# Second block: where the projections of its second attention, their head norms and its modulation stand in the order

## The reference

```
for l in range(2):
    mod = silu(c) @ w_ada[l] + b_ada[l]                 # 6 * 1024 values
    sh_m, sc_m, gt_m, sh_f, sc_f, gt_f = split(mod, 6)
    h = rms_norm(x, g_mix) * (1 + sc_m) + sh_m
    qa, ka, va, qi, ki, wi, qb, kb, vb, ga, gb = split_cols(h @ w_in + b_in)
    qa, ka = rope(rms_norm(..)) per head;  qi, ki = rope(..)
    # first attention: for each row the 128 best of the keys before it
    score = sum over 8 heads of wi * relu(qi . ki), masked
    sel   = top_k(score, 128)
    y_a   = (softmax(qa . ka over sel) @ va) @ w_oa     # 8 query heads, one key head
    # second attention: 8 heads, band mask and learned relative bias
    qb, kb = rms_norm(..) per head
    y_b   = (softmax(qb . kb + rel_bias) @ vb) @ w_ob
    x = x + gt_m * ((sigmoid(ga) * y_a + sigmoid(gb) * y_b) @ w_out)
    h2 = rms_norm(x, g_ffn) * (1 + sc_f) + sh_f
    x = x + gt_f * ((silu(gate) * up) @ w_down)
```

## Time and profile before

| what | value |
|---|---|
| median of 3 runs | 4852.56 us (4852.16 to 4854.54) |
| the profiled execution | 4852.07 us, its span 4850.2 us |
| mean granted clock of PE | 0.913 |
| PE busy | 4068.8 us (84% of the span) |
| DVE, ACT, POOL busy | 1387.2, 1445.4, 1428.4 us (29%, 30%, 29%) |
| chain that ended last | PE 77%, DVE 11%, ACT 4%, POOL 3%, issue 3%, DMA 2% |

### The profile page before, as it was taken

The page is one execution under the profiler, slowest core; times in us unless marked ns, Lnnn a source line. Parts: engine busy times, 40 slices in busy tenths (PEclk is TensorE's granted clock), DMA queues, the critical chain, the costliest instruction groups (busy, mean ns, idle before and its releaser), DMA issues.

```text
span 4850.2 us, 67804 instructions
## 1 busy us (share of the span) xinstructions
PE 4068.8 (84%) x28944; PEld 3207.1 (66%) x28944; DVE 1387.2 (29%) x2696; ACT 1445.4 (30%) x2476; POOL 1428.4 (29%) x617
## 2 busy tenths in 40 slices
PE   2898889899978878898997558897998567897998
PEld 2687568687756866786875335676886335676886
DVE  2443341311134533322112173213111163213111
ACT  1344142222223423432221213333221213333222
POOL 3200324544440012244443202233442201233443
PEclk9899899999989989998998668898999678898999
DMA  2000212122220001222223231121223231111222
GB/s 87 32 3 3 85 53 96 70 107 93 87 80 2 3 37 67 79 87 78 104 87 116 79 139 66 39 87 63 94 90 141 83 142 53 52 70 70 105 87 104
DMA packets 26699, 366.39 MB, mean 76 GB/s; under 512 B 3104, under 2 KB 3104, under 8 KB 4128
## 3 DMA queue, kind: packets, MB, share of 16 engines
q1 hardware_dynamic: 23040, 335.55, 18.6%
q10 hardware_dynamic: 3360, 26.47, 1.4%
HBM read 359.91 MB, written 2.10 MB: 75 GB/s over the span
## 4 chain that ended last, share of the span: by engine, by line
PE 77%; DVE 11%; ACT 4%; POOL 3%; issue 3%; DMA 2%; DVEq 0%; POOLq 0%; ACTq 0%; PEldq 0%; SPq 0%; PEld 0%
PE bank L579 20%; PE bank L580 20%; PE bank L581 19%; PE bank L850 10%; PE bank L1758 4%; ACT arena L1914 2%; DVE arena L2177 1%; DVE arena L2176 1%; ACT arena L1161 1%; PE bank L1861 1%; DMA ring<-stream 1%; DVE arena L1569 1%; POOL small L2035 1%; PE bank L1790 1%; DVE arena L1472 1%
## 5 line engine op out<-in xcount | busy, mean ns | idle before, releaser
L649 POOL TENSOR_TENSOR ring_r<-ring,hi_ring 128x1024 fp32r<-128x1024 f32 (+1 forms) x522 | 1252.5, 2402 | 2884.7 <-ACT hi_ring L640 2884.2
L579 PE MATMUL bank<-xT_r,ring_r 128*128 128x512 f32 x2288 | 915.5, 400 | 58.4 <-POOL ring_r L649 48.9
L580 PE MATMUL bank<-x_lo_r,hi_ring 128*128 128x512 f32 x2288 | 907.9, 397 | 0.0
L581 PE MATMUL bank<-xT_r,hi_ring 128*128 128x512 f32 x2288 | 903.9, 395 | 0.0
L640 ACT ACTIVATE hi_ring<-ring 128x1024 fp32r<-128x1024 f32 (+1 forms) x522 | 543.8, 1046 | 743.8 <-PE bank L581 396.9
L579 PEld LDWEIGHTS bank<-xT_r,ring_r 128*128 128x128 f32 x2288 | 437.5, 191 | 166.0 <-issue 67.8
L581 PEld LDWEIGHTS bank<-xT_r,hi_ring 128*128 128x128 f32 x2288 | 435.1, 190 | 101.3
L580 PEld LDWEIGHTS bank<-x_lo_r,hi_ring 128*128 128x128 f32 x2288 | 436.8, 191 | 95.8 <-issue 1.8
L850 PE MATMUL bank<-arena 64*64 64x64 f32 (+4 forms) x7456 | 393.7, 249 | 78.7 <-DVE arena L1472 29.7
L1161 ACT ACTIVATE arena<-bank 128x512 f32<-128x512 f32 (+1 forms) x422 | 230.7, 548 | 699.0 <-PE bank L581 493.3
L850 PEld LDWEIGHTS bank<-arena 64*64 64x64 f32 (+2 forms) x7456 | 304.9, 140 | 134.8 <-issue 91.4
(11 more groups left out here) (244 smaller groups left out, 4979.7 us busy)
## 6 DMA issues: line engine op xcount, KB each, us to landing
ring<-stream SPq DMA_DIRECT2D x160, 2048.0 KB, 7.7
arena<-pack ACTq DMA_DIRECT2D x2, 2564.0 KB, 10.4
arena<-ln_rows ACTq DMA_DIRECT2D x5, 1024.0 KB, 5.6
arena<-edge ACTq DMA_DIRECT2D x2, 2048.0 KB, 7.7
arena<-edge ACTq DMA_DIRECT2D x2, 1792.0 KB, 7.0
arena<-pack ACTq DMA_DIRECT2D x2, 1200.5 KB, 5.7
x<-x_in ACTq DMA_DIRECT2D x1, 2048.0 KB, 20.6
out<-x ACTq DMA_DIRECT2D x1, 2048.0 KB, 6.6
```

The lines of the kernel that those rows point to most:

```text
L579: first = nc.tensor.matmul(out_, left[1], right[0], start=start, stop=False)
L580: nc.tensor.matmul(out_, left[0], right[1], start=False, stop=False)
L581: return first, nc.tensor.matmul(out_, left[0], right[0], start=False, stop=stop)
L649: nc.gpsimd.tensor_tensor(feed.raw(n, ring_r), feed.raw(n), feed.hi(n).bitcast(F32), ALU.subtract).then_inc(split_lo, 1)
```

## The change

The list of steps of a layer of block 2 is written in another order, and buffers are moved so that this is free of overlaps.

- The head norm and rope of qa stand before the rows of qi, and the transposes of qa behind them; likewise those of qi stand behind the rows of misc. A step `head_scale` (the two scalings) is split from `head_norm`.
- The projections qb, kb and vb are cut into 48 parts (one piece, one row group: six products, `feed_row_part`). Six stand before the transposes of misc, two between the scores of each search round, 8, 13 and 15 behind the three searches. ACT copies their banks out (four copies each), and POOL adds the bias in one instruction of 128 x 2048 (step `bias`), which were four adds on DVE.
- No modulation stands in the search. Number 4 stands between search and first attention, and 5 to 11 in the first attention, each `mod_row` with its `mod_c` or `mod_g` right behind it in the same bank. The units in the stream are ordered to match.
- The head norms of qb and kb stand in rounds 2, 5, 12 and 15 of the first attention, the transposes of qb in rounds 8, 9, 10 and 12, those of kb in its last two.
- `crep` is made ahead of the wait for `pack`. `rel2` is loaded in two halves, at round 20 and at the end of the first attention. Four gate products, not three, stand in the second attention.

Cut to its core:

```diff
@@ -46,7 +46,8 @@
 DT = D // P
 RING = 2
 UNIT = 4096
-MOD_UNITS = (0, 1, 2, 3, 7, 8, 9, 10, 11, 12, 13, 14)
+MOD_UNITS = (0, 1, 2, 3, 10, 11, 12, 13, 14, 15, 16, 17)
+EARLY_GATES = 4
 ALPHA = (2.0 * L) ** 0.25
 LN_EPS = 1e-5
 KAPPA = math.exp(-0.5)
@@ -374,31 +375,52 @@
     for tt in range(TT):
         add("rms", 0, tt, banks=("power",))
         add("turn2", 0, tt, banks=(0, 1))
+    def turns_of(name, n, banks=(2, 3)):
+        for c in range(n):
+            add("rows_T", name, c, banks=(banks[c % len(banks)],))
+    rest = [(name, i, tt) for name in ("qb", "kb", "vb") for i in range(4) for tt in range(TT)]
+
+    def more(n):
+
+        for name, i, tt in rest[:n]:
+            if (i, tt) == (0, 0):
+                add("rows_open", name, banks=(4, 5, 6, 7))
+            add(*(("rows", name, i) if tt == 0 else ("rows_more", name, i, tt)))
+            if i == 3:
+                add("rows_out", name, tt)
+            if (i, tt) == (3, TT - 1):
+                add("bias", name)
+        del rest[:n]
     rows_of("qa")
     add("head_norm", "qa", banks=("power",))
+    add("head_scale", "qa")
     add("rope", "qa")
-    for c in range(4):
-        add("rows_T", "qa", c, banks=(2 + c % 2,))
-    rows_of("qi")
+    add("rows_open", "qi", banks=(4, 5, 6, 7))
+    for i in range(4):
+        add("rows", "qi", i)
+    turns_of("qa", 4)
+    for tt in range(TT):
+        add("rows_out", "qi", tt)
     add("rope", "qi")
-    for c in range(4):
-        add("rows_T", "qi", c, banks=(2 + c % 2,))
     rows_of("misc")
+    turns_of("qi", 4)
     add("head_norm", "ka", banks=("power",))
     add("rope", "misc")
-    for c in range(2):
-        add("rows_T", "misc", c, banks=(2 + c % 2,))
+    more(6)
+    turns_of("misc", 2)
     add("open_mask")
     for qt in range(1, TT):
         for h in range(HQ):
             add("idx", qt, h, banks=(h % 2,))
+            if h in (3, 5):
+                more(1)
         add("top", qt)
-
-        first = 2 + 2 * qt
-        for k in (first, first + 1):
-            add("mod_row", k, banks=(2 + k % 2,))
-        for k in (first, first + 1):
-            add("mod_g" if qt == 1 else "mod_c", k, banks=(4 + k % 2,))
+        more((8, 13, len(rest))[qt - 1])
+
+    def modulate(k, banks):
+        add("mod_row", k, banks=(banks[0],))
+        add("mod_g" if k in (4, 5, 10, 11) else "mod_c", k, banks=(banks[-1],))
+    modulate(4, (2, 3))
 
     def attend(a):
         add("s_qk", a, 0, banks=(2,))
@@ -407,10 +429,20 @@
                 add("s_qk", a, n + 1, banks=(2 + (n + 1) % 2,))
             if n < TT * HQ:
                 add("s_soft", a, n)
+            if a == 0 and n in (2, 12):
+                add("head_norm", ("qb", "kb")[n // 10], banks=("power",))
+            if a == 0 and n in (5, 15):
+                add("head_scale", ("qb", "kb")[n // 10])
             if 2 <= n < TT * HQ + 2:
                 add("s_tr", a, n - 2, banks=((4, 0)[n % 2],))
-            if a == 1 and n in (1, 11, 21):
-                add("gate", 0, n // 10, banks=(1,))
+            if a == 1 and n in (1, 9, 17, 25):
+                add("gate", 0, n // 8, banks=(1,))
+            if a == 0 and n % 4 == 3 and n < 28:
+                modulate(5 + n // 4, (1,))
+            if a == 0 and n in (8, 9, 10, 12):
+                add("rows_T", "qb", (8, 9, 10, 12).index(n), banks=(1,))
+            if a == 0 and n == 20:
+                add("rel_half")
             if n >= 3:
                 add("s_pv", a, n - 3)
             qt, h = divmod(n - 2, HQ)
@@ -418,21 +450,14 @@
...
-            if a == 0 and n in (4, 12):
-                add("mod_row", 10 + n // 8, banks=(1,))
-            if a == 0 and n in (6, 14):
-                add("mod_g", 10 + n // 8, banks=(1,))
+            if a == 0 and n in (32, 33):
+                for c in (0, 1):
+                    add("rows_T", "kb", 2 * (n - 32) + c, banks=(2 + c,))
     attend(0)
-    for name in ("qb", "kb"):
-        rows_of(name)
-        add("head_norm", name, banks=("power",))
-        for c in range(4):
-            add("rows_T", name, c, banks=(2 + c % 2,))
-    rows_of("vb")
...
@@ -458,14 +483,14 @@
...
-    return number(with_splits(out, second_pieces(), {12: ("rows_open", "qb")}))
+    return number(with_splits(out, second_pieces(), {24: ("mod_g", 11)}))
...
     for n, name in enumerate(("qb", "kb", "vb")):
-        out += row_pieces("rows", 15 + n, (name,))
+        out += row_pieces("rows", 7 + n, (name,))
@@ -682,6 +707,22 @@
             if i == 3:
                 last.then_inc(bank_full[banks[tt]], 1)
         if i < 3:
+            last.then_inc(piece_used, 1)
+
+    def feed_row_part(pe, feed, p, i, tt, b, left, begin):
+
+        if tt == 0:
+            pe.wait_ge(split_lo, p + 1)
+        release = begin(feed.unit(p))
+        w = feed.weights(p)
+        for t in range(2):
+            first, last = pair_product(bank[b][:, 0:w[0].shape[2]], [a[:, 2 * i + t, tt * P:(tt + 1) * P] for a in left],
+                                       [a[:, t, :] for a in w], i == 0 and t == 0, i == 3 and t == 1)
+            if release and t == 0:
+                first.then_inc(weights_used, 1)
+        if i == 3:
+            last.then_inc(bank_full[b], 1)
+        elif tt == TT - 1:
             last.then_inc(piece_used, 1)
 
     def feed_down(pe, feed, name, n, uses, begin):
@@ -1957,13 +2010,23 @@
...
-                act.wait_ge(staged, ["qa", "ka", "qb", "kb"].index(proj) + 1)
-                f(stage_sq.rearrange("p t c -> p (t c)"), stage.rearrange("p t c -> p (t c)"), ACT.Square)\
+                if proj == "qa":
+                    act.wait_ge(staged, 1)
+                else:
+                    act.wait_ge(biased, LATE.index(proj) + 1)
+                f(stage_sq[proj].rearrange("p t c -> p (t c)"), stage[proj].rearrange("p t c -> p (t c)"), ACT.Square)\
                     .then_inc(sums_sq, 1)
+            elif name == "rows_out" and args[0] in LATE:
+                proj, tt = args
+                b, n = [a[tt] for a in uses[("rows_open", proj)]]
+                filled(b, n)
+                f((vb if proj == "vb" else stage[proj])[:, tt, :], bank[b][:, :], ACT.Copy).then_inc(bank_free[b], 1)
+            elif name == "rel_half":
+                act.dma_start(arena[:, 15152:17200], edge2[bass.ds(layer * P, P), 0:HQ // 2 * S]).then_inc(rel_loaded, 16)
@@ -1995,7 +2058,7 @@
...
+                    act.dma_start(arena[:, 13104:15152], edge2[bass.ds(layer * P, P), HQ // 2 * S:HQ * S]).then_inc(rel_loaded_2, 16)
             elif name == "gate":
@@ -2027,6 +2090,12 @@
             banks, use = uses[(name,) + tuple(args)]
             if name == "split":
                 feed_gpsimd(pool, feed2, args[0])
+            if name == "bias":
+                proj = args[0]
+                drained(pool, uses, "rows_open", proj)
+                rows_ = vb if proj == "vb" else stage[proj]
+                nc.gpsimd.tensor_tensor(rows_, rows_, K2("b_rows", *ROWS[proj]).unsqueeze(1).to_broadcast([P, TT, S]), ALU.add)\
+                    .then_inc(biased, 1)
             if "power" not in banks:
                 continue
             n = use[banks.index("power")]
@@ -2048,9 +2117,9 @@
             def filled(b_=None, n_=None):
                 dve.wait_ge(bank_full[b if b_ is None else b_], (n if b_ is None else n_) + 1)
             if name == "params2":
-                dve.wait_ge(pack_loaded, 16)
                 V.tensor_copy(crep.rearrange("p (k c) -> p k c", k=DT), c_col.unsqueeze(2).to_broadcast([P, DT, 32]))\
                     .then_inc(crep_ready, 1)
+                dve.wait_ge(pack_loaded, 16)
                 link(V.tensor_scalar(half_bg, K2("b_gates"), 0.5, None, ALU.mult))
                 link(V.tensor_scalar(gain_qa, K2("qn_a"), 0.125, None, ALU.mult))
                 link(V.tensor_scalar(gain_qb, K2("qn_b"), 0.125, None, ALU.mult))
...
-                    dve.wait_ge(power_ready, n + 1)
-                    link(V.tensor_tensor(heads, heads, power.unsqueeze(2).to_broadcast([P, TT * HQ, CH]), ALU.mult))
-                    g_ = {"qa": gain_qa, "qb": gain_qb, "kb": K2("kn_b")}[proj]
-                    ins = V.tensor_tensor(heads, heads, g_.unsqueeze(1).to_broadcast([P, TT * HQ, CH]), ALU.mult)
...
+            elif name == "head_scale":
+                proj = args[0]
+                dve.wait_ge(power_ready, uses[("head_norm", proj)][1][0] + 1)
...
                 if i == 0 and a == 1:
-                    dve.wait_ge(rel_loaded, 16)
-                    for h_ in range(HQ):
-                        ins = V.memset(rel2[0:64, h_, S - CH:S], NEG)
-                    link(ins)
                     for c in (2, 3):
                         drained(dve, uses, "rows_T", "kb", c)
+                if i in (0, HQ // 2) and a == 1:
+                    dve.wait_ge((rel_loaded, rel_loaded_2)[i > 0], 16)
+                    for h_ in range(i, i + HQ // 2):
+                        ins = V.memset(rel2_at(h_)[0:64, S - CH:S], NEG)
```

(13 more changed lines are left out.)

92 lines of the change are left out of this document (47 added, 45 removed).

## The result

The changed kernel takes 4698.83 us (median of four runs, 4695.36 to 4702.31) against 4853.55 us (4852.16 to 4857.79): ratio 0.9683, 95% interval [0.9668, 0.9697]. That is 155 us less; I had forecast 178 less (4674 us, range 4615 to 4745).

A forecast was written before the change was run, and what follows sets the result against it. PE was taken as the bound, so only its waits and low clock could give. Terms of -113 + 9.5 - 19 - 8.5 + 40 + 2 = -89 us a layer, -178 for two, took 4852.07 to 4674 us, range 4615 to 4745.

The forecast's parts named there:

- the rival in which the modulations empty the attention: First attention: each modulation empties the pipeline of rounds and costs double, +65 a layer, 4724 us; chance 15%.
- The projections leave their place: Between the attentions: the 114 us stretch of projections goes, its products issued elsewhere, -113 us a layer.
- Their work under the search: Key search: projection parts hide under DVE's searches, with some delay from the POOL/DVE port, +9.5 us a layer.
- the rival in which the port blocks them: Key search: POOL's work also blocks maximum and replacement, search grows by 43 + 1 us, 4743 us; chance 10%.
- near 1 us: Start of the first attention: PE's wait for DVE was to be near 1 us instead of 21.
- Head norms and ropes behind the next projection: From qa to the search: waits for norms and ropes are hidden under the next projection's products, -19 us a layer.
- `crep`: Layer start: copied ahead of the parameters, it lets the first modulation products start earlier, -8.5 us a layer.
- The first attention: PE is its bound, so added modulations, transposes and norms add in full, +40 us a layer.
- Seven, two of them cold: +31: First attention: seven modulations at 3.75 us, about 6.2 for the two at the low clock, +31 us.
- the 9 us for the norms: First attention: of 14 to 16 us of DVE head norms, some 9 stay on the path after buffered rounds.
- The rival of the low clock: Search and first attention: PE stays at 1.2 GHz until the attention's end, +30 us a layer, 4913 us; chance 4%.
- The second attention: The fourth gate only moves forward and the second half of `rel2` may be late, +2 us a layer.

The follow-up runs named there:

- no_bias: The changed kernel with the three bias additions on POOL cut to 8 columns, the rest left out: 4681.71 us.
- crep_first: The kernel before the change with one edit, DVE copying `crep` before it waits for the parameters: 4836.28 us, ratio 0.9961.
- apart: The changed kernel with the small products of modulations 5 to 11 two rounds behind their mod_rows instead of right behind: 4664.06 us.
- after: The changed kernel itself, with the whole change and no further edit: 4698.83 us.
- quarters: apart with the head norms of qb and kb cut by row tile and the transposes of qb moved with them: 4647.43 us.
- before_together: The kernel before the change, its two first-attention modulations with the small product right behind mod_row: twelve runs, 4858.4 to 4942.2 us.
- before: The kernel without the change, which the changed one is compared with: 4853.55 us.
- apart_no_norms: apart with the head norms of qb and kb left out: 4621.37 us.

## Why the prediction was right, and where not

The direction, the place of the gain and the range were right, and the time 25 us too low; it lies halfway to the rival in which the modulations empty the attention (4724).

*The projections leave their place.* -113.0 and -112.3 measured. A stretch that goes away as a whole is the safest term.

*Their work under the search.* +7.8 and +8.7 against +9.5, and for the reason given. Maximum and replacement took 562 and 542 ns in a search in which POOL was busy for 31 us, and 561 and 541 in one without POOL, so the rival in which the port blocks them is out. The weighted sums paid 7.5 us, where I had 8.5; no_bias takes 5.8 of it back. The Trainium skill ("SBUF — State Buffer", Who interferes with whom) draws the line there, between instructions with two inputs in SBUF and with one, and the trace agrees (4.73 us against 0.75 for the first kind, no change for the second). My "near 1 us" for PE's wait at the attention's start was wrong, it is 6.2: vb's parts and modulation 4 run out before the third search does.

*Head norms and ropes behind the next projection.* -22.0 and -17.8 against -19, the clock 0.98 where it was 0.82.

*`crep`.* -10.0 and -10.2 against -8.5; alone, in crep_first, 12 to 25 us for both layers.

*The first attention.* This is the step that failed: "That is 41.8, and as a little of the norms will fall into the pauses of the modulations I take 40." It is +57.4. The counts were right, and so was the pause (0.81 us in six of seven, for 0.75). What was mis-sized is "Seven, two of them cold: +31": five were cold and a sixth for the most part, and not they alone but the rounds between them. I had priced a pause at its own length. apart, with the same work and no pause, has 102.8 us, +37; the other 20 us a layer, 40 in all, hang on the pause, and they are work at 1.2 GHz rather than waiting. Two smaller terms were off too: of the 9 us for the norms only 2.6 show as waits in after (in apart 10), and the 4 us for a late unit of modulation 5 don't show at all. The attentions came out 35 us over in the two layers; that the total is only 25 off is luck, since the other terms gave 10 more than I had set. The rival "the modulations empty the attention" had the size (+65) and not the mechanism, since PE waits there for only 11 us. The rival of the low clock had the mechanism, but I had argued against it from a stretch where gates stand among sparse rounds, at 0.91. That mean hides a fall to 0.50 between the first and the second gate, without a pause; the gates are dense, and the clock is high again behind the second.

Neither mark that I had set for being wrong was reached: the attention took 123 us (130), the search 97 (120). But the attention was to be near 105 us at a clock over 0.85, and it took 123 at 0.69.

*The second attention.* +0.5 and +0.6 against +2. Both halves of `rel2` were there in time: DVE waited for no DMA in it.

## What to carry to other kernels

Where PE is busy and sparse, read the granted clock by stretch before adding up durations: the same attention took 65.6 us at 0.94 or, with one product moved, 105.7 at 0.56. Let no product wait for the copy of the dense one just before it, if other work can stand between; two rounds between them were worth 35 us of 4699 here. And cut long instructions of a helper engine to the length that its buffers bridge: quarters was 17 us quicker than apart.

## What the runs showed of the hardware

- PE at 1.2 GHz stayed there through 84 us in which it was busy for 83 (before_together), and at 2.4 GHz through 56 in which it was busy for 54.5 (before). The Trainium skill ("TensorE: Matmul & The Clock Gate", Part 1) says that a monitor sets the clock by how busy the engine has been. If the busy time of the profile's records were what it looks at, both should have been at 2.4 GHz; they were not, so that busy time does not foretell the clock here.
- Leaving out seven mod_rows, seven small products and the pauses made apart slower, 4677 against 4664 us, with the clock of the attention at 0.53 instead of 0.85.
- Moving one small product (two modulations of each layer) turned a kernel whose 17 runs agree within 11 us into one whose 12 runs lie at three times, 40 us apart.
- A weighted sum of 128x512 on DVE took 4.73 us instead of 0.75 beside a POOL addition of 128x2048 (4.65 us); maximum and replacement beside POOL took no longer.
- The clock of a stretch can change with work left out elsewhere: the second attention took 86.4 us at 0.92 in after and apart, and 80.3 at 1.00 in apart_no_norms, with the same instructions in it.
